# 128 bytes more ahead of the experts' token and activation buffers in a two-layer trunk (GLA, retention, SwiGLU, experts)

## The chip, the core and the metric

The kernel runs on one core of one Trainium2 chip. The metric is the device time of one execution in microseconds (us); lower is better. Three runs of the kernel before took 1833.35, 1835.13 and 1835.06 us, median 1835.06.

## What is computed

256 tokens of 1,024 features, with 16 learned meta tokens ahead of them (272 in all), go through two layers. Each layer has two attention-like branches merged by gates, a norm, then a channel mixer and a second norm. The mixer is a dense SwiGLU in the first layer and eight experts, of which each token uses two, in the second. Cut to the part that the change touches:

```python
def swiglu(x, w_gate, w_up, w_down):
    return (jax.nn.silu(x @ w_gate) * (x @ w_up)) @ w_down

def moe_swiglu(x, w_router, w_gate, w_up, w_down):
    t = x.reshape(-1, d)
    probs = jax.nn.softmax((t @ w_router).astype(jnp.float32), axis=-1)
    top_p, top_i = lax.top_k(probs, TOP_K)
    top_p = top_p / jnp.sum(top_p, axis=-1, keepdims=True)
    combine = jnp.sum(jax.nn.one_hot(top_i, N_EXPERTS) * top_p[..., None], axis=1)
    for e in range(N_EXPERTS):
        out = out + combine[:, e:e + 1] * swiglu(t, w_gate[e], w_up[e], w_down[e])
    return out
```

All inputs are float32. An expert's three matrices are 1024 x 3584, 1024 x 3584 and 3584 x 1024.

## The kernel before

**Split products.** Every large product is made of three float32r matmuls. An operand is split into a high half, which ScalarE (ACT) makes by a copy to float32r, and a low half, which VectorE (DVE) makes as operand less high half. `mm3` (lines 763 to 765) adds weights-low x stream-high, weights-high x stream-low and high x high into one PSUM tile. In the names of the trace, `ps<-w_hi,xg_lo` has the streamed tile first and the tile whose columns are loaded as weights second. "Loaded as weights" is meant here as TensorE's: the operand that LDWEIGHTS puts into the array.

**Units.** Weight matrices come from memory in units of 128 x 2048 float32 (1 MB). SyncE issues a load into one of `RAW` = 6 slots of `raw` when VectorE is done with the unit that was there (`lo_ready`). ACT writes the unit's high half into one of `HALVES` = 3 slots of `w_hi`, as soon as TensorE is done with the unit three before (`units_used`); VectorE then writes `w_lo`; TensorE waits for `lo_ready` before the unit's first matmul, and a unit is 12 matmuls of 512 columns in the experts.

**Dense stages** (layer 0, and layer 1 up to the router). The model's matrices are loaded as weights, 128 columns at a time (`w_hi`, `w_lo`), and the tokens are streamed: `hT`, `zT`, `mT`, `aT`, each with 272 columns, or with 256, which begin 16 columns (64 bytes) later.

**Experts.** The roles are swapped. An expert's tokens are gathered by one-hot matmuls into `xg_hi`, `xg_lo` (two experts per gather), and 128 of their columns at a time are loaded as weights, while 512 columns of the expert's matrix are streamed. The hidden dimension has 7 chunks of 512. A chunk of an expert is, on TensorE, in `chunk` (line 1139 and on): the gate, 2 units (24 matmuls, lines 763 to 765); the turn, four transposes of the activations `a_sl` of the chunk before (line 1086); the up, 2 units (24 matmuls, lines 763 to 765); and the down, 2 units (24 matmuls, lines 1101 to 1104), whose weights are the turned activations of the chunk before, `ag_hi` and `ag_lo`. After the turn, ACT does in program order: `ag_hi` (line 1231, called from `turned`), the gate's SiLU `g_sl` (line 1475), and then the `w_hi` of the two units of the down. VectorE does `ag_lo` (line 2107), the `w_lo` of the down's units (line 1820), and the product `a_sl` (line 2117) between them. There are 8 experts, so 56 chunks. Each engine's order is written out by hand, and nothing in it depends on addresses.

**Where the tiles lie.** Tensors are placed one behind another in each SBUF partition, each at the next multiple of 32 bytes. Three of the unnamed pads (`row_start`, `hidden_start`, `tokens_start`) only move what follows them. Byte addresses in a partition, from the built program:

| tile | role | address before | modulo 256 | after, modulo 256 |
|---|---|---|---|---|
| w_hi, w_lo (slots of 8,192) | weights in dense, stream in experts | 53,376; 77,952 | 128 | 128 |
| hT_hi, hT_lo (rows of 1,280 per k) | dense stream | 115,776; 126,016 | 64 | 64 |
| zT_hi, zT_lo (rows of 1,088 per k) | dense stream | 196,576; 205,280 | 224, 32, 96, 160 with k | same |
| aT_hi, aT_lo (rows of 1,280 per k) | dense stream (FFN) | 145,984; 174,144 | 64 | 64 |
| x_hi, x_lo | weights in the gathers | 145,984; 154,176 | 64 | 192 |
| S | stream in the gathers | 162,368 | 64 | 192 |
| xg_hi, xg_lo | weights in gate and up | 165,440; 173,632 | 64 | 192 |
| g_sl, a_sl | SiLU, activations | 181,824; 183,872 | 64 | 192 |
| ag_hi, ag_lo | weights in down | 185,920; 187,968 | 64 | 192 |
| y_hi, y_lo | stream in the last scatter | 190,016; 194,112 | 64 | 192 |

Steps within a tile are 2,048 bytes per k in w_hi and w_lo and 512 per k in xg and ag, all multiples of 256.

Of the kernel before, what the change touches and what calls it, by code (L numbers as in the profile page):

```python
# [28 lines left out]
P = 128  # L29
# [166 lines left out]
def trunk(nc, w, consts, where, out):  # L196

    ctx = ExitStack()
    with ctx:
# [3 lines left out]
        def sb(stack, name, shape, dt=F32):  # L203
            return stack.enter_context(nc.sbuf_tensor(name, shape, dt))
# [99 lines left out]


        moe = ExitStack()
        sb(moe, "tokens_start", [P, 24])
        x_hi = sb(moe, "x_hi", [P, 2, D], F32R)
        x_lo = sb(moe, "x_lo", [P, 2, D], F32R)
        S = sb(moe, "S", [P, 2, 2, P], F32R)  # L310
# [1983 lines left out]
```

How the kernel before makes its waits and increments, by code:

```python
        def landed(eng, u):  # L435
            eng.wait_ge(raw_landed[u % RAW], 16 * (u // RAW + 1))
# [2 lines left out]
        def hi_unit(act, u):  # L440
            landed(act, u)
            if u >= HALVES:
                act.wait_ge(units_used, u - HALVES + 1)
            k, n = shape_of(u)
            nc.scalar.activation(w_hi[:, u % HALVES, 0:k * n], raw[:, u % RAW, 0:k * n], ACT.Copy).then_inc(hi_ready, 1)
# [1 line left out]
        def lo_unit(dve, u):  # L447
            dve.wait_ge(hi_ready, u + 1)
            if u >= HALVES:
                dve.wait_ge(units_used, u - HALVES + 1)
            k, n = shape_of(u)
            if stream[u][0] == "twice":
                second = [unit(a, i, k, n).rearrange("p k (q i r) -> p (k q) i r", i=2, r=RANK)[:, :, 1, :] for a, i in ((w_hi, u % HALVES), (raw, u % RAW))]
                nc.vector.tensor_tensor(second[0], second[1], second[0].bitcast(F32), ALU.subtract).then_inc(lo_ready, 1)
                return
            nc.vector.tensor_tensor(w_lo[:, u % HALVES, 0:k * n], raw[:, u % RAW, 0:k * n],
                                    w_hi[:, u % HALVES, 0:k * n].bitcast(F32), ALU.subtract).then_inc(lo_ready, 1)
# [1 line left out]
        def lo_half(dve, u, q):  # L459
            if q == 0:
                dve.wait_ge(hi_ready, u + 1)
                dve.wait_ge(units_used, u - HALVES + 1)
            these = slice(q * UNIT // 2, (q + 1) * UNIT // 2)
            nc.vector.tensor_tensor(w_lo[:, u % HALVES, these], raw[:, u % RAW, these], w_hi[:, u % HALVES, these].bitcast(F32),
```

## Time and profile before

| what | value |
|---|---|
| median of the three runs | 1835.06 us |
| the profiled execution | 1834.15 us |
| its span, first to last instruction | 1832.1 us |
| TensorE matmuls | 10,888, busy 1792.3 us (98%) |
| VectorE | busy 1367.0 us (75%) |
| ScalarE | busy 1097.3 us (60%) |
| memory traffic | 498.61 MB, mean 272 GB/s |
| granted TensorE clock, mean | 0.993 of full speed |

The profile's page gives the busy time of every engine, a picture of the span in 40 slices, the chain of work that ended last, and the costliest groups of instructions with their mean durations. Matmuls are pipelined: their records overlap, so the pace of TensorE is read from the starts of neighbouring matmuls in the timeline and not from their durations. In the timeline the first column is the start in us from the start of the span, the second the duration.

### The profile page before, as it was taken

How to read it: one execution, taken by the hardware profiler on the slowest of the kernel's cores; microseconds unless marked ns; L12 is line 12 of the kernel's file. 1: busy time of each engine (PE TensorE's matmuls, PEld its weight loads, DVE VectorE, ACT ScalarE, POOL GpSimd, SP SyncE). 2: the span in 40 equal slices, each digit the busy share in tenths (PEclk: the TensorE clock that was granted, in tenths of full speed). 3: DMA queues.
4: the chain of work that ended last, by engine and by line, in shares of the span. 5: the costliest groups of instructions: out<-in, count | busy, mean ns of one | idle time of the engine just before them, and what ended most of it. 6: DMA issues, size and time to landing. Idle time of an engine off the chain costs nothing.

```text
span 1832.1 us, 28131 instructions
## 1 busy us (share of the span) xinstructions
PE 1792.3 (98%) x10888; PEld 1591.6 (87%) x10888; DVE 1367.0 (75%) x1159; ACT 1097.3 (60%) x840; POOL 74.3 (4%) x141
## 2 busy tenths in 40 slices
PE   8999999999999999999999999999999999999996
PEld 8999999999989999998878888888888888888875
DVE  4756577545457466668888888888888888888887
ACT  5544354543345442647777777777677777777774
POOL 0300200000003002000000000000000000000100
PEclk9999999999999999998999999999999999999998
DMA  8635443545535455344999999999999999999993
GB/s 334 209 133 168 163 162 138 184 148 186 185 138 194 150 187 187 131 175 164 370 364 380 366 347 379 364 381 379 348 369 369 365 383 372 349 371 371 397 395 131
DMA packets 75826, 498.61 MB, mean 272 GB/s; under 512 B 11072, under 2 KB 11584, under 8 KB 17872
## 3 DMA queue, kind: packets, MB, share of 16 engines
q1 hardware_dynamic: 68304, 482.38, 69.7%
q0 software_dynamic: 5824, 11.55, 2.0%
q10 hardware_dynamic: 1600, 3.31, 0.7%
q8 instruction: 69, 1.13, 0.3%
q14 instruction: 29, 0.24, 0.0%
HBM read 485.83 MB, written 4.72 MB: 268 GB/s over the span
## 4 chain that ended last, share of the span: by engine, by line
PE 55%; DVE 2%; issue 2%; ACT 1%; DVEq 0%; ACTq 0%
PE ps L763 12%; PE ps L765 12%; PE ps L764 12%; PE ps L1101 5%; PE ps L1103 5%; PE ps L1104 5%; PE ps L1086 1%; DVE w_lo L1820 1%; PE ps L1123 1%; ACT w_hi L1231 1%; PE ps L1034 0%; PE ps L1043 0%; PE ps L941 0%; PE ps L945 0%; DVE a_sl L2117 0%
## 5 line engine op out<-in xcount | busy, mean ns | idle before, releaser
L1820 DVE TENSOR_TENSOR w_lo<-raw,w_hi 128x2048 fp32r<-128x2048 f32 x336 | 762.8, 2289 | 127.2 <-ACT w_hi L1231 125.7
L1231 ACT ACTIVATE w_hi<-raw 128x2048 fp32r<-128x2048 f32 x336 | 638.3, 1918 | 177.6 <-PE ps L1104 89.6
L456 DVE TENSOR_TENSOR w_lo<-raw,w_hi 128x2048 fp32r<-128x2048 f32 (+2 forms) x126 | 272.5, 2171 | 195.2 <-ACT w_hi L445 194.6
L763 PE MATMUL ps<-hT_hi,w_lo 128*128 128x272 f32 (+1 forms) x1376 | 396.2, 288 | 15.4 <-DVE w_lo L456 8.1
L765 PE MATMUL ps<-hT_hi,w_hi 128*128 128x272 f32 (+1 forms) x1376 | 394.1, 286 | 0.0
L764 PE MATMUL ps<-hT_lo,w_hi 128*128 128x272 f32 (+1 forms) x1376 | 394.0, 286 | 0.0
L763 PE MATMUL ps<-w_hi,xg_lo 128*128 128x512 f32 x896 | 357.8, 399 | 2.4 <-DVE w_lo L1820 2.4
L765 PE MATMUL ps<-w_hi,xg_hi 128*128 128x512 f32 x896 | 351.3, 392 | 0.0
L764 PE MATMUL ps<-w_lo,xg_hi 128*128 128x512 f32 x896 | 350.1, 391 | 0.0
L445 ACT ACTIVATE w_hi<-raw 128x2048 fp32r<-128x2048 f32 (+2 forms) x130 | 234.2, 1807 | 179.2 <-PE ps L765 141.6
L763 PEld LDWEIGHTS ps<-hT_hi,w_lo 128*128 128x128 f32 x1376 | 261.1, 190 | 17.9 <-DVE w_lo L456 8.1
L764 PEld LDWEIGHTS ps<-hT_lo,w_hi 128*128 128x128 f32 x1376 | 261.1, 190 | 0.1
L765 PEld LDWEIGHTS ps<-hT_hi,w_hi 128*128 128x128 f32 x1376 | 261.0, 190 | 0.0
L765 PEld LDWEIGHTS ps<-w_hi,xg_hi 128*128 128x128 f32 x896 | 168.2, 188 | 38.9
L763 PEld LDWEIGHTS ps<-w_hi,xg_lo 128*128 128x128 f32 x896 | 168.5, 188 | 38.0 <-DVE w_lo L1820 2.5
L764 PEld LDWEIGHTS ps<-w_lo,xg_hi 128*128 128x128 f32 x896 | 168.5, 188 | 34.2
L1101 PE MATMUL ps<-w_hi,ag_lo 128*128 128x512 f32 x440 | 176.3, 401 | 0.0
L1103 PE MATMUL ps<-w_lo,ag_hi 128*128 128x512 f32 x440 | 172.5, 392 | 0.0
L1104 PE MATMUL ps<-w_hi,ag_hi 128*128 128x512 f32 x440 | 172.1, 391 | 0.0
L1101 PEld LDWEIGHTS ps<-w_hi,ag_lo 128*128 128x128 f32 x440 | 82.6, 188 | 28.0 <-DVE w_lo L1820 9.2
L1104 PEld LDWEIGHTS ps<-w_hi,ag_hi 128*128 128x128 f32 x440 | 82.6, 188 | 19.0
L1103 PEld LDWEIGHTS ps<-w_lo,ag_hi 128*128 128x128 f32 x440 | 82.7, 188 | 15.7
(306 smaller groups left out, 1813.0 us busy)
## 6 DMA issues: line engine op xcount, KB each, us to landing
raw<-in_dense_units SPq DMA_DIRECT2D x116, 1024.0 KB, 4.9
raw<-in_moe_w_gate SPq DMA_DIRECT2D x112, 1024.0 KB, 7.3
raw<-in_moe_w_up SPq DMA_DIRECT2D x112, 1024.0 KB, 7.1
raw<-in_moe_w_down SPq DMA_DIRECT2D x112, 1024.0 KB, 7.1
raw<-in_dense_units SPq DMA_DIRECT2D x10, 512.0 KB, 3.8
result_rows<-rows POOLq DMA_DIRECT2D x7, 512.0 KB, 8.6
v_tok<-turned_v POOLq DMA_DIRECT2D x48, 64.0 KB, 2.8
srT<-o_tok ACTq DMA_DIRECT2D x6, 272.0 KB, 4.6
```

The source lines that it names most:

```text
L445: nc.scalar.activation(w_hi[:, u % HALVES, 0:k * n], raw[:, u % RAW, 0:k * n], ACT.Copy).then_inc(hi_ready, 1)
L456: nc.vector.tensor_tensor(w_lo[:, u % HALVES, 0:k * n], raw[:, u % RAW, 0:k * n], w_hi[:, u % HALVES, 0:k * n].bitcast(F32), ALU.subtract) ...
L763: nc.tensor.matmul(dst, l_lo, r_hi, start=start, stop=False)
L764: nc.tensor.matmul(dst, l_hi, r_lo, start=False, stop=False)
L765: return nc.tensor.matmul(dst, l_hi, r_hi, start=False, stop=stop)
L1086: last = nc.tensor.transpose(TB[:, i * P:(i + 1) * P], a_sl[:, i * P:(i + 1) * P], ident)
L1101: last = nc.tensor.matmul(Y[:, q, :], a_lo[:, 2 * i + kk, :], u_hi[:, o:o + COLS], start=first and i == 0 and kk == 0, stop=False)
L1103: nc.tensor.matmul(Y[:, q, :], a_hi[:, 2 * i + kk, :], u_lo[:, o:o + COLS], start=False, stop=False)
L1104: last = nc.tensor.matmul(Y[:, q, :], a_hi[:, 2 * i + kk, :], u_hi[:, o:o + COLS], start=False, stop=final and i == 1 and kk == 1)
L1123: last = nc.tensor.matmul(ps[1 - half][:, 2 + k // 2, (k % 2) * 2 * P:(k % 2 + 1) * 2 * P], x_[:, t, f:f + P], S[:, t, :, :].rearrange("p ...
L1231: return nc.scalar.activation(dst, src, ACT.Copy, **kw)
L1820: tt(w_lo[:, at % HALVES, :], raw[:, at % RAW, :], w_hi[:, at % HALVES, :].bitcast(F32), ALU.subtract).then_inc(lo_ready, 1)
```

## The change

The pad ahead of the experts' buffers grows from 24 to 56 float32 per partition, so that all tensors that are allocated behind it in the experts' part of SBUF begin 128 bytes further on. Tensors of the dense stages, which share that memory at other times, and `raw`, `w_hi` and `w_lo` keep their addresses. No instruction is added, removed or moved on any engine.

```diff
         moe = ExitStack()
-        sb(moe, "tokens_start", [P, 24])
+        sb(moe, "tokens_start", [P, 56])
         x_hi = sb(moe, "x_hi", [P, 2, D], F32R)
         x_lo = sb(moe, "x_lo", [P, 2, D], F32R)
         S = sb(moe, "S", [P, 2, 2, P], F32R)
```

## Rows read from the trace of the kernel before

**Rows 1.** The page, busy time and share of the span.

```profile
span 1832.1 us, 28131 instructions
...
PE 1792.3 (98%) x10888; PEld 1591.6 (87%) x10888; DVE 1367.0 (75%) x1159; ACT 1097.3 (60%) x840; POOL 74.3 (4%) x141
```

**Rows 2.** Busy time by stage: PE, PEld, DVE, ACT, POOL, clock, DMA share, GB/s.

```profile
1000.00:1700.00 700.00, 700.00 (x3169) 570.99 (x3168) 605.04 (x348) 511.45 (x342) 2.67 (x5) 1.00 0.96 368
...
1700.00:1740.00 40.00, 40.00 (x179) 32.54 (x178) 34.89 (x20) 29.86 (x20) 8.85 (x5) 1.00 1.00 403
```

**Rows 3.** Timeline of PE, one chunk: down, gate, turn, up, next down.

```profile
1404.44 0.45 PE L1101 MATMUL ps<-w_hi,ag_lo 128*128 128x512 f32 x1
...
1405.88 0.39 PE L1101 MATMUL ps<-w_hi,ag_lo 128*128 128x512 f32 x1
...
1414.81 0.39 PE L763 MATMUL ps<-w_hi,xg_lo 128*128 128x512 f32 x1
...
1415.51 0.60 PE L1086 MATMUL ps<-tab,a_sl 128*128 128x128 f32 x4
...
1421.22 0.40 PE L765 MATMUL ps<-w_hi,xg_hi 128*128 128x512 f32 x1
1421.46 0.45 PE L1101 MATMUL ps<-w_hi,ag_lo 128*128 128x512 f32 x1
1421.75 0.39 PE L1103 MATMUL ps<-w_lo,ag_hi 128*128 128x512 f32 x1
```

**Rows 4.** Timeline of PE, the same instructions in another chunk.

```profile
1300.08 0.40 PE L1103 MATMUL ps<-w_lo,ag_hi 128*128 128x512 f32 x1
...
1309.41 0.40 PE L765 MATMUL ps<-w_hi,xg_hi 128*128 128x512 f32 x1
```

**Rows 5.** Timeline of PE, dense stages: ends of four stretches of 48 spacings.

```profile
57.84 0.28 PE L765 MATMUL ps<-hT_hi,w_hi 128*128 128x272 f32 x1
...
63.76 0.28 PE L765 MATMUL ps<-hT_hi,w_hi 128*128 128x272 f32 x1
...
627.75 0.28 PE L763 MATMUL ps<-hT_hi,w_lo 128*128 128x256 f32 x1
...
633.51 0.28 PE L763 MATMUL ps<-hT_hi,w_lo 128*128 128x256 f32 x1
...
265.93 0.29 PE L765 MATMUL ps<-zT_hi,w_hi 128*128 128x272 f32 x1
...
271.95 0.29 PE L765 MATMUL ps<-zT_hi,w_hi 128*128 128x272 f32 x1
...
775.81 0.28 PE L764 MATMUL ps<-zT_lo,w_hi 128*128 128x256 f32 x1
...
781.49 0.28 PE L764 MATMUL ps<-zT_lo,w_hi 128*128 128x256 f32 x1
```

**Rows 6.** The costliest groups: busy us, mean ns, idle before and its releaser.

```profile
L1820 DVE TENSOR_TENSOR w_lo<-raw,w_hi 128x2048 fp32r<-128x2048 f32 x336 | 762.8, 2289 | 127.2 <-ACT w_hi L1231 125.7
L1231 ACT ACTIVATE w_hi<-raw 128x2048 fp32r<-128x2048 f32 x336 | 638.3, 1918 | 177.6 <-PE ps L1104 89.6
...
L763 PE MATMUL ps<-w_hi,xg_lo 128*128 128x512 f32 x896 | 357.8, 399 | 2.4 <-DVE w_lo L1820 2.4
...
L1101 PE MATMUL ps<-w_hi,ag_lo 128*128 128x512 f32 x440 | 176.3, 401 | 0.0
```

**Rows 7.** Timelines of ACT, DVE and PEld from the turn to the down.

```profile
1416.15 0.60 ACT L1231 ACTIVATE ag_hi<-ps 128x512 fp32r<-128x512 f32 x1 [1.28 <-PE ps L1086]
1416.64 0.59 ACT L1475 ACTIVATE g_sl<-ps 128x512 f32<-128x512 f32 x1
1417.12 3.71 ACT L1231 ACTIVATE w_hi<-raw 128x2048 fp32r<-128x2048 f32 x2
...
1419.07 4.49 DVE L1820 TENSOR_TENSOR w_lo<-raw,w_hi 128x2048 fp32r<-128x2048 f32 x2 [1.27 <-ACT w_hi L1231]
...
1421.41 0.19 PEld L1101 LDWEIGHTS ps<-w_hi,ag_lo 128*128 128x128 f32 x1 [0.22 <-DVE w_lo L1820]
```

**Rows 8.** Waits from 850 us on: total us, times, longest.

```profile
PEld ps L1101 <- DVE w_lo L1820: 9.2, 42, 0.2
```

## The prediction

> **What bounds the kernel now.** I read the page first. TensorE's matmul row is busy for 98% of the span [rows 1], so time is to be looked for between one matmul's start and the next. Then the table by stage: from 1000 to 1700 us, inside the experts, PE is busy all 700 us at the full granted clock (1.00, which is the 2.4 GHz level), with VectorE at 605 us and DMA at 0.96 and 368 GB/s [rows 2]. A busy PE says nothing of its pace, because each matmul's record (about 0.39 us) overlaps the next. The pace is in the starts, so the third view is the timeline of one chunk of an expert. Call the distance from one matmul's start to the next its spacing. From 1405.88 to 1414.81 us there are 39 spacings: 8.93 us / 39 = 229.0 ns [rows 3]. The 512 streamed columns at 2.4 GHz are 213.3 ns, so 15.7 ns of each matmul is something else. In another chunk the same instructions go at 233.3 ns (1300.08 to 1309.41, 40 spacings in 9.33 us) [rows 4]: two steady paces for one code, 4.3 ns apart. Four of the 56 chunks go at the slower pace from down to gate; one stands here for them.
>
> The dense stages show what that rest may be. Four stretches of 48 spacings each [rows 5]: with hT streamed, 272 columns, 5.92 us / 48 = 123.3 ns, 10.0 over the 113.3 of its columns; with hT, 256 columns, 5.76 / 48 = 120.0, 13.3 over 106.7; with zT, 272 columns, 6.02 / 48 = 125.4, 12.1 over; with zT, 256 columns, 5.68 / 48 = 118.3, 11.6 over. Same engine, same kind of operand, same clock. What differs is where the operands lie. While one matmul streams, the next one's weights are loaded, so for each pair I take the **distance**: start address of the weights being loaded less the start of the columns being streamed, modulo 256 bytes. From the table of addresses it is +64 in the first stretch (128 - 64), 0 in the second (its stream begins 16 columns, 64 bytes, later), and goes round +160, +96, +32, +224 with k in the two of zT, whose rows of 1,088 bytes are no multiple of 256. In the experts the roles are swapped: the stream is w_hi or w_lo (128), the weights are xg or ag (64), the distance is -64, that is 192, and the rest is the largest of all, 15.7 or 20.0.
>
> The Trainium skill (TensorE: Matmul & The Clock Gate, Part 2, the step on LDWEIGHTS) says that PE has two independent read ports into SBUF, so that loading the next weights takes no read bandwidth from the running matmul, and its Part 1 gives a start to start of N / 2.4 GHz plus about 2.5 ns, 215.7 ns for 512 columns. By that rule addresses could not matter; the trace disagrees on the pace, with 229.0 ns.
>
> **The change, part by part.**
>
> 1. *No instruction is added, removed or moved.* Every engine's order is the same, and nothing ahead of the router touches a moved buffer: 0 us.
>
> 2. *The gates, ups and downs.* They are 56 chunks of 72 matmuls, 4,032 in all: 896 on each of the three lines of the gates and ups, and on each of the three lines of the downs 440 [rows 6] and 8 more of the last down, whose weights lie in xg. Their stream stays at 128, their weights go from 64 to 192, so the distance goes from 192 to +64, which is what the first stretch has now. No row shows 512 columns at +64. Bounds: the best neighbour is that stretch itself, 10.0 over, so 213.3 + 10.0 = 223.3 ns; the worst is the pace that these very matmuls already fall into, 233.3 ns. I take 225.0, that is 11.7 over: the mean of the four dense stretches (10.0, 13.3, 12.1, 11.6 make 11.75). I don't take 10.0, because two stretches that differ in columns and distance together can't tell me which of the two made the 10.0.
>
> 3. *What of it reaches the end.* A chunk is gate (24 matmuls), a turn of four transposes, up (24), down (24). From the turn at 1415.51 to the first down at 1421.46 PE does not set the time [rows 3]. The chain there is [rows 7]: the turn ends, ACT writes ag_hi from 1416.15, g_sl from 1416.64, then w_hi from 1417.12 (1.92 us for the first of the two [rows 6]), VectorE the w_lo of it from 1419.07 for 2.29 us [rows 6] to 1421.36, and the down's weight load starts at 1421.41 with 0.22 us of idle time ended by that w_lo. The waits add up to 9.2 us over 42 times [rows 8]. So an up phase that runs faster only waits longer: its 1,344 matmuls give nothing. The margin is thin: the first down comes 0.24 us after the last up matmul, one ordinary spacing, and its successor 0.29 us later in place of 0.23, so the wait costs PE about 0.06 us a chunk, 3.4 us in 56. The other 48 matmuls of a chunk (down, then gate) have no such tie: 1404.44 to 1415.51, 11.07 us. Their w_lo come in time: the table of waits has no other line by which w_lo holds PE for over 3 us of the stage.
>    Gain: 56 x 48 = 2,688 matmuls x (229.0 - 225.0) = 10.8 us, and the four slow chunks give 4 x 48 x 4.3 = 0.8 us more. **11.6 us**.
>
> 4. *Who must follow.* A chunk goes from 17.02 to 16.8 us. From 1000 to 1700 us VectorE is busy 605 of 700 us and ACT 511 [rows 2], which is 14.7 and 12.4 us of a chunk. Six units of 1.049 MB in 16.8 us are 374 GB/s, and from 1700 to 1740 us the queues moved 403 [rows 2]. I cost these at 0. If that cover failed, DMA kept at 368 GB/s would give the whole 11.6 back.
>
> 5. *The small ones.* The 224 transposes, 128 gathers and 8 scatter matmuls: in the gathers stream and weights (S and x) move together, distance 0 before and after. ACT and VectorE write ag, xg and a_sl at new places; nothing in the trace tells that an address matters to them. 0, with a bound of half a microsecond either way.
>
> Sum: span 1832.1 - 11.6 = 1820.5; the profiled execution took 1834.15, 2.05 over its span, so 1822.5; the median of the runs shown, 1835.06, lies 0.9 above that execution, so **1823.5 us**.
>
> **The rivals.**
>
> *Nothing changes.* The pattern of places may repeat every 128 bytes, and then +64 and -64 are one place; or the rest of 15.7 ns comes from the 512 columns and not from the distance. For it: hT's k step, 1,280 bytes, is a multiple of 128 as well as of 256, and the steady rows don't tell the two apart; 15.7 is outside what any dense stretch has, as if length had a part in it. Against: the two steady dense stretches differ by 3.3 ns, and zT's wander with k. Time: 1835. The Trainium skill's rule of the two read ports (same page and step) would end here too.
>
> *The slower pace becomes the usual one.* The stream and the load fall into step with each other, and the new distance may favour the step that now takes 4 chunks of 56. The 2,688 down and gate matmuls then take 233.3: 2,688 x 4.3 = 11.6, less 0.8 for the chunks that already do. The up phase becomes longer by 1,344 x 4.3 = 5.8, but the first 3.4 of it fills the wait for w_lo. Together +13.2 us: 1848. It decides from 230.4 ns on: 1.4 ns on 2,688 matmuls are 3.7 us, while the up phase's 1.9 still vanish in the wait. For it: the pace exists, with the same instructions. Against: it is the rarest in the trace, and the distance of the coming layout has the shortest rest in the dense stage.
>
> *The up phase was not pinned.* If the chain of ACT and VectorE shortened too, all 4,032 would gain 4.0 ns, 16 us, and 1818. Against it stands [rows 7]: none of the four durations depends on PE's pace.
>
> **How the numbers follow.** A measurement of this kernel can tell 0.2%, 3.7 us, from no change; in down and gate that is 1.4 ns a matmul. Faster by more, at 223 to 227 ns: 0.50, the up phase unpinned within it at 0.03. No change: 0.24. Slower: 0.26, of which the full slower pace is some 0.12 and a pace between 230 and 233 the rest. The forecast is the likeliest case, 1823.5. Its own range is 1818 (223.3 ns: 2,688 x 5.7 + 0.8 = 16.1) to 1831. The whole range has to reach into the slower cases, so 1817 to 1848.
>
> **What the profile after would show.** The time up to the first gate's matmul the same to 1 us. In a chunk, 39 spacings from down into gate in 8.78 us (225.0) and not 8.93. From the turn to the first down still 5.95 us, with the waits of the down's weight load for w_lo grown from 9.2 us to about 9.2 + 56 x 24 x 0.0040 = 14.6 us. VectorE's and ACT's mean durations unchanged (2.29, 1.92 us). DMA near 372 GB/s in the stage. Wrong would be: a chunk's spacings at 229.0 (no change), at 231 or more (the slower pace), or the time from turn to first down itself shorter.

## The result, and the profile after

| | before, same chip | after |
|---|---|---|
| median | 1834.38 us | 1845.07 us |
| lowest to highest, 4 runs each | 1833.35 to 1835.13 | 1843.73 to 1846.01 |
| the profiled execution, its span | 1834.15, 1832.1 | 1846.01, 1844.2 |

The change makes the kernel slower: the ratio is 1.0055, with a 95% interval of 1.0043 to 1.0068, that is 10.7 us in the difference of the medians. The forecast was 1823.5 us, faster; the sign was wrong. The time lies inside the stated range, 2.9 us under the 1848 of the rival "the slower pace becomes the usual one".

The page of the kernel after, its span, busy shares and three of its groups, beside [rows 1, 6]:

```profile
span 1844.2 us, 28131 instructions
...
PE 1804.6 (98%) x10888; PEld 1593.7 (86%) x10888; DVE 1367.0 (74%) x1159; ACT 1099.2 (60%) x840; POOL 74.4 (4%) x141
...
L1820 DVE TENSOR_TENSOR w_lo<-raw,w_hi 128x2048 fp32r<-128x2048 f32 x336 | 762.8, 2289 | 137.9 <-ACT w_hi L1231 137.2
L1231 ACT ACTIVATE w_hi<-raw 128x2048 fp32r<-128x2048 f32 x336 | 640.2, 1919 | 183.5 <-PE ps L765 92.9
...
L763 PE MATMUL ps<-w_hi,xg_lo 128*128 128x512 f32 x896 | 359.4, 401 | 1.9 <-DVE w_lo L1820 1.9
```

The same instructions, and VectorE's and ScalarE's durations are unchanged (2289 ns, 1919 ns): the new addresses of what they write cost them nothing. A matmul's record is as long as before, 401 ns against 399. Nothing on the page names the cause. It tells only that PE is busy 12.3 us longer in a span that is 12.1 us longer.

Busy time by stage of the kernel after (PE, PEld, DVE, ACT, POOL, clock, DMA share, GB/s):

```profile
1000.00:1700.00 700.00, 700.00 (x3133) 565.46 (x3132) 598.11 (x345) 506.31 (x337) 2.68 (x5) 1.00 0.95 363
1700.00:1740.00 40.00, 40.00 (x180) 32.09 (x178) 34.46 (x19) 29.19 (x21) 8.70 (x5) 1.00 0.98 388
```

Against [rows 2] the same 700 us hold 3,133 matmuls and not 3,169, at the same granted clock of 1.00. DMA moves 363 GB/s where it moved 368, and VectorE idles more: they follow.

Timeline of PE after, one chunk, with the same rows as [rows 3]:

```profile
1406.43 0.60 PE L1086 MATMUL ps<-tab,a_sl 128*128 128x128 f32 x4
...
1412.24 0.40 PE L765 MATMUL ps<-w_hi,xg_hi 128*128 128x512 f32 x1
1412.47 0.40 PE L1101 MATMUL ps<-w_hi,ag_lo 128*128 128x512 f32 x1
1412.71 0.39 PE L1103 MATMUL ps<-w_lo,ag_hi 128*128 128x512 f32 x1
...
1413.87 0.39 PE L1101 MATMUL ps<-w_hi,ag_lo 128*128 128x512 f32 x1
...
1422.96 0.40 PE L763 MATMUL ps<-w_hi,xg_lo 128*128 128x512 f32 x1
```

From 1413.87 to 1422.96 there are 39 spacings from down into gate: 9.09 us / 39 = 233.1 ns, where before it was 229.0. That is the slower pace of [rows 4], and now all chunks go at it: from the fourth spacing of a phase on, the mean is 233.3 ns in gates, ups and downs alike. From the turn to the first down it is 6.04 us and was 5.95. The second down follows the first by 0.24 us, close to an ordinary spacing, where it was 0.29: the wait for `w_lo` is gone. The chain around it, timelines of ACT, DVE and PEld after, beside [rows 7]:

```profile
1407.07 0.60 ACT L1231 ACTIVATE ag_hi<-ps 128x512 fp32r<-128x512 f32 x1 [1.32 <-PE ps L1086]
1407.57 0.59 ACT L1475 ACTIVATE g_sl<-ps 128x512 f32<-128x512 f32 x1
1408.04 3.75 ACT L1231 ACTIVATE w_hi<-raw 128x2048 fp32r<-128x2048 f32 x2
...
1409.99 4.49 DVE L1820 TENSOR_TENSOR w_lo<-raw,w_hi 128x2048 fp32r<-128x2048 f32 x2 [1.32 <-ACT w_hi L1231]
...
1412.34 0.19 PEld L1101 LDWEIGHTS ps<-w_hi,ag_lo 128*128 128x128 f32 x1
```

The down's weight load at 1412.34 shows no idle time, while VectorE had the `w_lo` ready at about 1412.28 (1409.99 + 2.29). The row of [rows 8], 9.2 us over 42 times, is no longer among the waits, and the later run "The change on top of it", which makes that `w_lo` earlier still, leaves turn to first down at 6.04. So ups that go slower have used up the slack of that chain and now set the time themselves.

**Where the 10.7 us came from.** I added up the spacings of the experts' matmuls over all chunks. A spacing goes to the phase of its first matmul. "All" is the three phases and the last down (6.0 us, not in the column of the downs); the turns (19.9 us before and after) and the gathers are left out:

| us | gates | ups | downs | all |
|---|---|---|---|---|
| before | 308.97 | 314.45 | 309.45 | 938.8 |
| after | 314.12 | 318.68 | 310.89 | 949.7 |
| difference | +5.2 | +4.2 | +1.4 | +10.9 |

The downs grow by only 1.4 us because in them the vanished wait pays back: at the first spacing of the downs 2.65 us over all chunks, at the last spacing of the ups 0.47. The other 1.3 of the span's 12.1 us lie ahead: the first expert matmul starts at 844.6 us before and at 845.9 after, and the gather ahead of it is late by the same 1.3 us already (842.68 and 843.93). In the kernels below, whose instructions up to there are the same, the first expert matmul starts anywhere from 843.5 to 845.5, in no order of the distances, so I take this part for scatter between executions.

### The profile page after: what moved, and what is told of

It reads as the page before. It is cut to its first block, busy times and chain, and to the rows that moved or that the text cites. A ratio compares the mean times of both kernels' runs of the same rounds, so it can differ in the third digit from the quotient of the medians.

```text
span 1844.2 us, 28131 instructions
## 1 busy us (share of the span) xinstructions
PE 1804.6 (98%) x10888; PEld 1593.7 (86%) x10888; DVE 1367.0 (74%) x1159; ACT 1099.2 (60%) x840; POOL 74.4 (4%) x141
## 4 chain that ended last, share of the span: by engine, by line
PE 55%; DVE 2%; issue 2%; ACT 1%; DVEq 0%; ACTq 0%
PE ps L763 12%; PE ps L765 12%; PE ps L764 12%; PE ps L1101 5%; PE ps L1103 5%; PE ps L1104 5%; PE ps L1086 1%; DVE w_lo L1820 1%; PE ps L1123 1%; ACT w_hi L1231 0%; PE ps L1034 0%; PE ps L1043 0%; PE ps L941 0%; PE ps L945 0%; ACT g_sl L1475 0%
## 5 line engine op out<-in xcount | busy, mean ns | idle before, releaser
L1820 DVE TENSOR_TENSOR w_lo<-raw,w_hi 128x2048 fp32r<-128x2048 f32 x336 | 762.8, 2289 | 137.9 <-ACT w_hi L1231 137.2
L1231 ACT ACTIVATE w_hi<-raw 128x2048 fp32r<-128x2048 f32 x336 | 640.2, 1919 | 183.5 <-PE ps L765 92.9
L764 PE MATMUL ps<-w_lo,xg_hi 128*128 128x512 f32 x896 | 353.8, 395 | 0.0
L445 ACT ACTIVATE w_hi<-raw 128x2048 fp32r<-128x2048 f32 (+2 forms) x130 | 234.2, 1807 | 180.0 <-PE ps L765 141.9
```

The lines of the kernel that those rows point to most:

```text
L445: nc.scalar.activation(w_hi[:, u % HALVES, 0:k * n], raw[:, u % RAW, 0:k * n], ACT.Copy).then_inc(hi_ready, 1)
L764: nc.tensor.matmul(dst, l_hi, r_lo, start=False, stop=False)
L1231: return nc.scalar.activation(dst, src, ACT.Copy, **kw)
L1820: tt(w_lo[:, at % HALVES, :], raw[:, at % RAW, :], w_hi[:, at % HALVES, :].bitcast(F32), ALU.subtract).then_inc(lo_ready, 1)
```

## The experiments

All times are medians beside runs of the kernel before on the same chip. "Distance" is, as in the prediction, the start of the weights being loaded less the start of the streamed columns, modulo 256 bytes; -64 stands for 192 here. Edits are against the kernel before unless the text says otherwise.

### Which property of the addresses counts

**One full period further.** The theory takes addresses modulo 256.

```diff
-        sb(moe, "tokens_start", [P, 24])
+        sb(moe, "tokens_start", [P, 88])
```

> The pad is 88 instead of 24 float32, so the experts' tiles begin 256 bytes further on than before, again at 64 modulo 256. Theory D (the pace of the 512-column matmuls depends on the distance modulo 256 between the start of the weights being loaded and the start of the columns being streamed): distance 192 as before, spacing 229 ns in most chunks and 233.3 in a few, time 1835 within 0.2%. If instead any move of these tiles costs (a boundary that is crossed, or a period longer than 256 bytes), the spacing stays at 233.3 ns and the time near 1845 us.

Measured: 1834.52 us beside 1835.06, ratio 1.000 (0.999 to 1.0009). The pace of a chunk is 229.0 again (1422.93 to 1431.86, 39 spacings). That the tiles lie further on does nothing; 128 bytes more make the loss, 256 bytes more undo it.

**Everything 128 further.** Stream and weights move together, so the distance stays -64 while every place modulo 256 is a new one.

```diff
+        sb(ctx, "all_start", [P, 32])
         raw = sb(ctx, "raw", [P, RAW, UNIT])
```

> A pad of 32 float32 ahead of raw moves every tile by 128 bytes, streams and weights alike; tokens_start is 24 as before. The experts' weights now lie at 192 modulo 256 as in the changed kernel, and their streams at 0. Theory D (distance): every distance is as before, so 229 ns in the experts, 123.3 and 120.0 in the dense stretches, time 1835 within 0.2%. Theory A (the absolute place of the weights' tile, 192 instead of 64, sets the pace): 233.3 ns in the experts and 1845 us.

Measured: 1835.07 us beside 1835.06, ratio 1.0001 (0.9991 to 1.001), pace 229.0. It is the distance between the two operands, and not the place of either. This is the run that bears out step 2's choice of variable.

**The turned activations alone.** Only `g_sl`, `a_sl`, `ag_hi`, `ag_lo` and what lies behind them move; gates and ups keep -64, downs get +64.

```diff
         xg_lo = sb(moe, "xg_lo", [P, 2, KT, P], F32R)
+        sb(moe, "hidden_half_start", [P, 32])
         g_sl = sb(moe, "g_sl", [P, COLS])
```

> A pad of 32 float32 behind xg_lo moves g_sl, a_sl, ag and all behind them by 128 bytes, while x, S and xg stay. Distance +64 in the downs alone. Theory D: downs at 233.3 ns, gates and ups at 229 (unless a gate keeps the pace that the down before it fell into, as nothing stops PE between them; the up begins afresh after the turn and tells it). Time between: about a third of the 10.7 us, 1838; two thirds if the gates keep the downs' pace, 1842. If the moved writes of ACT and VectorE (g_sl, a_sl, ag) and not TensorE's reads made the loss, the whole of it, 1845, at unchanged gates.

Measured: 1840.02 us beside 1835.06, ratio 1.0028 (1.0018 to 1.0038). In the timeline of PE of this run the pace changes inside one chunk, at the line between down and gate (its lines are numbered one higher):

```profile
1409.21 0.39 PE L1102 MATMUL ps<-w_hi,ag_lo 128*128 128x512 f32 x1
...
1413.88 0.39 PE L1105 MATMUL ps<-w_hi,ag_hi 128*128 128x512 f32 x1
...
1414.81 0.39 PE L764 MATMUL ps<-w_hi,xg_lo 128*128 128x512 f32 x1
...
1419.39 0.39 PE L766 MATMUL ps<-w_hi,xg_hi 128*128 128x512 f32 x1
```

Twenty spacings each: 4.67 / 20 = 233.5 ns in the downs, whose weights moved, and 4.58 / 20 = 229.0 in the gates, whose weights did not. It is so in most chunks, but not in all. Of the 53 downs that a gate follows directly, all go at 233 ns; of the gates behind them 37 go at 229, 15 at 233 and one between, where in the kernel before 4 go at 233. So a gate can keep the slower pace of the down ahead of it although its own distance has not changed, as the expectation allowed for. By the sum over starts that makes the gates 1.3 us longer, which fits a time between its 1838 and 1842. Behind a turn, the ups are at 229 in all 56 chunks.

**The tokens alone.** The change, and behind `xg_lo` another 128 bytes, which bring the activations back to where they were modulo 256.

```diff
-        sb(moe, "tokens_start", [P, 24])
+        sb(moe, "tokens_start", [P, 56])
...
         xg_lo = sb(moe, "xg_lo", [P, 2, KT, P], F32R)
+        sb(moe, "hidden_half_start", [P, 32])
```

> The complement of e3: x, S and xg at 192 modulo 256 as in the changed kernel, g_sl, a_sl and ag put back to 64 by a second pad of 32 behind xg_lo. Distance +64 in gates and ups, -64 in downs. Theory D: gates and ups at 233.3 ns, downs at 229 and partly at 233.3 where they keep the pace; the up phase 4.3 us longer in sum as in the changed kernel, the gates 5.2, less the wait at the first down (3.1): about 6 us, 1841. With e3's 5.0 that adds up to the change's 10.7. If xg's writers or the gathers made the loss, gates and ups stay at 229.

Measured: 1841.61 us beside 1834.14, ratio 1.0037 (1.0024 to 1.005). By the sum over starts the gates are 5.0 us longer and the ups 4.3, while the downs are 2.4 shorter, since their wait is gone and their pace stayed at 229.6 (229.3 before). The two halves cost 1.0028 and 1.0037 where the whole costs 1.0055: the effect follows the operand, but for the gates that keep their downs' pace in the run above.

### Which distance does what

**The map.** Behind the last scatter, extra matmuls run in groups of 48 (16 times `mm3`) on tiles that are there anyway; nothing of the output comes from them. The weights start at a place in `hT` that is chosen per group, the stream starts at the start of `w_hi` and `w_lo`.

```diff
+            def pace(off, n, triples=16):
+                x_h, x_l = hT_hi[:, 1, off:off + P], hT_lo[:, 1, off:off + P]
+                for i in range(triples):
+                    mm3(ps[0][:, 0, 0:n], x_h, x_l, w_hi[:, 0, 0:n], w_lo[:, 0, 0:n], start=(i == 0), stop=(i == triples - 1))
+            for n in (512, 272, 256):
+                for off in range(0, 64, 8):
+                    for _ in range(2):
+                        turned_idle()
+                        pace(off, n)
```

> Behind the last scatter PE runs 48 stretches of 48 matmuls: 512, 272 and 256 columns streamed from w_hi and w_lo (128 modulo 256), weights from hT_hi and hT_lo at eight starts 32 bytes apart, distances -64, -32, 0, +32, +64, +96, +128, +160, each twice, four transposes ahead of each. It is extra work at the end, some 0.5 ms; the output is the same. Theory D: the spacing depends on the distance and repeats what the kernel shows: 512 columns 229 at -64 and 233.3 at +64, 272 columns 123.3 at +64, 256 columns 120.0 at 0. If length alone made the experts' larger rest, 512 columns would have one spacing at all eight. The map says whether a distance with under 229 ns exists.

Six stretches of its timeline of PE, 39 spacings each. In this order: 512 columns at the distances -64, 0 and +64, then 272 columns at +64, then 256 columns at 0 and at +64.

```profile
1838.90 0.39 PE L765 MATMUL ps<-w_hi,hT_hi 128*128 128x512 f32 x1
...
1847.83 0.40 PE L765 MATMUL ps<-w_hi,hT_hi 128*128 128x512 f32 x1
...
1873.61 0.39 PE L765 MATMUL ps<-w_hi,hT_hi 128*128 128x512 f32 x1
...
1882.45 0.40 PE L765 MATMUL ps<-w_hi,hT_hi 128*128 128x512 f32 x1
...
1919.60 0.39 PE L765 MATMUL ps<-w_hi,hT_hi 128*128 128x512 f32 x1
...
1928.70 0.40 PE L765 MATMUL ps<-w_hi,hT_hi 128*128 128x512 f32 x1
...
2063.76 0.29 PE L765 MATMUL ps<-w_hi,hT_hi 128*128 128x272 f32 x1
...
2068.57 0.29 PE L765 MATMUL ps<-w_hi,hT_hi 128*128 128x272 f32 x1
...
2139.45 0.28 PE L765 MATMUL ps<-w_hi,hT_hi 128*128 128x256 f32 x1
...
2144.12 0.28 PE L765 MATMUL ps<-w_hi,hT_hi 128*128 128x256 f32 x1
...
2170.13 0.28 PE L765 MATMUL ps<-w_hi,hT_hi 128*128 128x256 f32 x1
...
2174.55 0.28 PE L765 MATMUL ps<-w_hi,hT_hi 128*128 128x256 f32 x1
```

8.93 / 39 = 229.0; 8.84 / 39 = 226.7; 9.10 / 39 = 233.3; 4.81 / 39 = 123.3; 4.67 / 39 = 119.7 (120.0 by unrounded times); 4.42 / 39 = 113.3 ns. The whole map, in ns of a spacing over the time of the columns at 2.4 GHz (two values where the two repeats differ by over half a ns):

| distance | 512 columns | 272 | 256 |
|---|---|---|---|
| -64 | 15.6 or 20.0 | 13.3 | 11.1 |
| -32 | 20.0 | 12.5 | 10.0 |
| 0 | 13.3 | 12.1 | 13.3 |
| +32 | 20.0 | 12.0 or 13.3 | 11.7 |
| +64 | 20.0 | 10.0 | 11.1 or 6.7 |
| +96 | 20.9 | 9.9 | 12.1 or 10.7 |
| 128 | 19.9 or 19.1 | 13.3 | 12.0 |
| 160 | 20.0 | 12.0 | 13.3 |

The 20.0 at -64 is its first repeat. It began while the granted clock was at 0.50, the 1.2 GHz level, with matmuls 427 ns apart; when the clock rose in it, the rest of the group settled at 233.4 ns (1828.21 to 1836.38, 35 spacings), and the second repeat, begun at the full clock, at 229.0. So the two paces of [rows 4] and [rows 3] are there for one distance in this run too. That the beginning of a stretch decides between them is a guess from this one pair; the first repeat also had the last of the kernel's DMA traffic beside it (71 GB/s from 1828 to 1838 us, then none). This is the table that the prediction needed. Its column for 272 columns agrees with the dense stage, where +64 is among the best, 10.0 as in [rows 5]. Its column for 512 has another order: there +64 is as bad as nearly all others, -64 is the second best, and 0 is the best. The kernel before sat on one of the two good places that this map has at its own length, and the change moved it off.

**Other lengths.** The same extra work at 512, 448, 384, 320 and 256 columns, with 160 transposes ahead of the first group.

> A second map behind the last scatter, each stretch of 48 matmuls twice, 40 turns of transposes ahead so that the clock is up: 512 columns at distances -64, -48, -16, 0, +16, +48, +64, and 448, 384, 320 and 256 columns at -64, 0, +64. Extra work at the end; the output is the same. Open is why +64 gives 10.0 ns over the columns at 272, 11 or 6.7 at 256 and 20.0 at 512. Theory L1: the length modulo 64 columns (256 bytes) decides with the distance; then 448, 384 and 320 give 512's rests (15.6, 13.3, 20.0). Theory L2: the rest grows with the length, because the stream and the load disturb each other over a part of the stream; then +64 goes from about 11 at 256 to 20 at 512 through values between. If distances of 16 bytes either side of 0 are above 13.3, 0 is a narrow optimum; if below, a better place than 0 exists.

| over the columns, ns | -64 | 0 | +64 |
|---|---|---|---|
| 512 | 15.6 | 13.3 | 20.0 |
| 448 | 13.3 | 16.0 or 20.0 | 15.5 |
| 384 | 13.3 | 13.3 | 16.7 |
| 320 | 13.3 | 13.3 | 13.4 |
| 256 | 11.1 | 13.3 | 6.7 |

At 512 columns -48 gave 18.6, -16 gave 13.3 in one repeat and 15.0 in the other, and +16 and +48 20.0. I had thought of the columns' number modulo 64 as what turns the order round; all but 272 are multiples of 64 here and still don't agree, so that idea fell. At +64 the rest grows from 6.7 at 256 columns to 20.0 at 512, with 448 out of line. No simple rule in length and distance holds for the whole table. The values between 256 and 512 columns speak for a rest that grows with the length at this one distance, as theory L2 of the expectation has it, and against L1. At -64 it grows too (11.1, 13.3, 15.6), but at 0 it is 13.3 at every length except 448. Two repeats of the same group can settle at different paces here also. At -64 and 512 columns both repeats took 228.9 ns this time.

**Distance 160 in the kernel.** Is it the sign of the distance, or are -64 and 0 special? The tokens' tiles go to 32 modulo 256, so the distance is -96, that is 160.

```diff
-        sb(moe, "tokens_start", [P, 24])
+        sb(moe, "tokens_start", [P, 16])
```

> The pad is 16: the experts' tiles at 32 modulo 256 and not at 64, distance -96, that is +160. The map gave 233.33 ns there. Theory D with the map: the chunks at 233.3 and the time like the changed kernel's, 1845. If it is only the sign of the distance that matters (weights behind their stream good, ahead of it bad), -96 should be like -64, 229 ns and 1835.

Measured: 1845.53 us beside 1834.54, ratio 1.006 (1.0045 to 1.0076), pace 233.3 (1413.57 to 1422.67). It moves the tiles by 32 bytes and costs as much as the change does with 128. The map's 20.0 at 160 holds in the kernel.

**Distance 0 in the kernel.** The best place of the map.

```diff
-        sb(moe, "tokens_start", [P, 24])
+        sb(moe, "tokens_start", [P, 40])
```

> The pad is 40: the experts' tiles begin 64 bytes further on than before, at 128 modulo 256 like their streams, distance 0. Theory D with the map: 226.7 ns in place of 229.0 in down and gate, 2,688 x 2.3 = 6.2 us and 0.8 from the slow chunks; the up phase is pinned by the chain ACT, VectorE, down (turn to first down stays 5.95 us) and gives nothing: about 1828 us. If the up phase was not pinned, 10.1 us, 1825. A theory in which any step away from 64 harms, or in which the changed kernel's loss came from something else than the distance, gives 1835 or more.

Measured: 1828.91 us beside 1834.14, ratio 0.997 (0.9959 to 0.9982). Timeline of PE of this run, from down into gate, then the following turn:

```profile
1418.60 0.39 PE L1101 MATMUL ps<-w_hi,ag_lo 128*128 128x512 f32 x1
...
1427.44 0.39 PE L763 MATMUL ps<-w_hi,xg_lo 128*128 128x512 f32 x1
...
1428.12 0.60 PE L1086 MATMUL ps<-tab,a_sl 128*128 128x128 f32 x4
...
1434.03 0.50 PE L1101 MATMUL ps<-w_hi,ag_lo 128*128 128x512 f32 x1
1434.37 0.39 PE L1103 MATMUL ps<-w_lo,ag_hi 128*128 128x512 f32 x1
```

39 spacings in 8.84 us: 226.7 ns, the map's number. The first down comes 5.91 us behind the turn and was at 5.95; the second comes 6.25 behind it and was at 6.24. So what the chain of `w_lo` holds in place is the second down, not the first: the mean from the turn to the second down, over the 50 chunks whose turn, up, down and next gate follow without a gather between, is 6.25 us in the kernel before and 6.25 here. The wait has grown; its row among the waits from 850 us on:

```profile
PEld ps L1101 <- DVE w_lo L1820: 10.7, 42, 0.3
```

This is step 3 of the prediction in a kernel that did become faster. By the sums, gates win 3.5 us, ups only 1.4, and downs 0.6, since their first spacing now takes 316 ns at the median and took 292: over all chunks 1.5 us more, which is all that the ups won. The ups win less than 24 x 2.3 ns a chunk for a reason of their own, too: 28 of the 56 go at 231 ns for about their first ten spacings and at 227 from then on, and with the wait taken away (below, distance 0 and the swap) 27 do so still.

### What the wait for w_lo costs

**The wait taken away alone.** ACT makes the high half of the down's first unit ahead of the gate's SiLU and that of the second behind it; `w_lo` is then ready before the down needs it.

```diff
                     turned(k - 1, uj)
+                    hi_of(g, 8, turns, uj + 4)
                     silu(k, uj + 2)
-                    for i in range(4, 6):
-                        hi_of(g, 4 + i, turns, uj + i)
+                    hi_of(g, 9, turns, uj + 5)
```

> The kernel before with the swap of e6 alone, tiles at 64. Theory P: the up phase keeps its 229 ns and only the wait at the first down goes, 3.4 us: 1831.6. The difference between e4 to e6 and this one is then what the pin took from a shorter spacing. Against P: no change, 1835.

Measured: 1828.2 us beside 1834.14, ratio 0.9968 (0.9956 to 0.998). The timeline of PE around the end of the ups:

```profile
1412.49 0.60 PE L1086 MATMUL ps<-tab,a_sl 128*128 128x128 f32 x4
...
1418.21 0.39 PE L765 MATMUL ps<-w_hi,xg_hi 128*128 128x512 f32 x1
1418.44 0.39 PE L1101 MATMUL ps<-w_hi,ag_lo 128*128 128x512 f32 x1
1418.67 0.39 PE L1103 MATMUL ps<-w_lo,ag_hi 128*128 128x512 f32 x1
```

The second down comes 0.23 us after the first. From the turn to the first down it is 5.95 us as in the kernel before: with the wait gone, turn and ups alone take that long. To the second down it is 6.18 in place of 6.24. The wait was priced at 3.4 us and the edit gives 5.9. By position within the phases, over all chunks, the wait itself shows as 3.2 us at the first spacing of the downs, 0.8 at the last of the ups, and 0.5 at the second and third of the downs: 4.5 us. Another 1.0 us lies at the step from the down to the gate, and there nearly all of it in four places: 1268, 820, 817 and 1025 ns became 1065, 493, 495 and 815. The first three are gates that wait for their own `w_lo`, the fourth is the step to the last down. So the swap shortens other waits with the first. The row of the gates' wait before, and in this run:

```profile
PE ps L763 <- DVE w_lo L1820: 2.4, 5, 0.9
```

```profile
PE ps L763 <- DVE w_lo L1820: 1.0, 2, 0.7
```

The rest is in ordinary spacings, of which fewer go at the slower pace (in the downs a mean of 228.9 ns, and 229.3 before).

**The change on top of it.** With the slack gone, nothing should absorb a slower up.

```diff
-        sb(moe, "tokens_start", [P, 24])
+        sb(moe, "tokens_start", [P, 56])
...
                     turned(k - 1, uj)
+                    hi_of(g, 8, turns, uj + 4)
                     silu(k, uj + 2)
-                    for i in range(4, 6):
-                        hi_of(g, 4 + i, turns, uj + i)
+                    hi_of(g, 9, turns, uj + 5)
```

> The changed kernel (pad 56, distance +64) with the swap of e6. Theory: in the changed kernel the wait at the first down was already gone, so the swap gives it nothing: 1845. Against e7, the same at distance -64, the loss is then that of all 4,032 matmuls with nothing absorbed, 4,032 x 4.35 = 17.5 us (1828.2 to about 1845.5), where the change alone cost 10.7. If the swap helps by another way than the wait, it gives some 6 us here too, 1839.

Measured: 1842.94 us beside 1834.54, ratio 1.0049 (1.0033 to 1.0064). Against the run before it, which has the swap alone, the ratio is 1.0049 / 0.9968 = 1.0081, 14.9 us, where the change alone costs 10.7. So the wait hid about 4 us of the slower pace. The 17.5 us of the expectation were too many, since it counted every spacing of every phase. By the sum over starts the two kernels differ by 15.6 us, and the first three spacings of the ups are no slower in this one. With the slower pace the swap is worth next to nothing: 1.0049 and 1.0055 have intervals that overlap. In the trace it still gives 1.3 us at the same four steps out of a down.

### The version that beats both

**Distance 0 and the swap.** The two edits of above together.

> e4, and in ScalarE's chunk the SiLU is issued behind the first w_hi of the down and not ahead of it. Theory P (the up phase is pinned by ag_hi, SiLU, w_hi, w_lo): that w_lo is ready some 0.5 us sooner, the wait at the first down goes, 0.06 us x 56 = 3.4 us, and the up phase gains 1,344 x 2.3 = 3.1 us of its own: about 6.5 us below e4, 1821 to 1822. If e4 shows the up phase unpinned, or if the chain is held by something else (ag_lo on VectorE, the load), no gain over e4.

Measured: 1819.1 us (1819.0 to 1820.64) beside 1834.14, ratio 0.992 (0.9906 to 0.9933). Its timelines of PE and of ACT:

```profile
1408.60 0.60 PE L1086 MATMUL ps<-tab,a_sl 128*128 128x128 f32 x4
...
1414.53 0.39 PE L1101 MATMUL ps<-w_hi,ag_lo 128*128 128x512 f32 x1
1414.75 0.39 PE L1103 MATMUL ps<-w_lo,ag_hi 128*128 128x512 f32 x1
...
1425.41 0.60 PE L1086 MATMUL ps<-tab,a_sl 128*128 128x128 f32 x4
```

```profile
1409.23 0.60 ACT L1231 ACTIVATE ag_hi<-ps 128x512 fp32r<-128x512 f32 x1 [1.24 <-PE ps L1086]
1409.72 1.91 ACT L1231 ACTIVATE w_hi<-raw 128x2048 fp32r<-128x2048 f32 x1
1411.54 0.58 ACT L1475 ACTIVATE g_sl<-ps 128x512 f32<-128x512 f32 x1
```

Turn to first down 5.93 us, to the second 6.15, first down to next turn 10.88, where the kernel before has 5.95, 6.24 and 11.07. In ACT's rows the `w_hi` stands ahead of `g_sl`, which puts the down's `w_lo` 0.5 us earlier. The gains of the two edits alone, 0.3% and 0.3%, give 0.8% together: each uncovers what the other left. The expectation had 1821 to 1822; it counted the wait at 3.4 us.

**The dense stream moved too.** On top of that version `hT` begins 32 bytes earlier modulo 256.

```diff
-        sb(ctx, "row_start", [P, 48])
+        sb(ctx, "row_start", [P, 40])
...
-        sb(ctx, "after_a2", [P, 48])
+        sb(ctx, "after_a2", [P, 56])
```

> e6 and hT_hi, hT_lo 32 bytes nearer (row_start 40, after_a2 56): distance +96 where hT streams 272 columns and +32 where 256. The map: 123.3 ns at +96 like at +64, and 118.4 at +32 in place of 120.0 at 0. Theory D: the 864 matmuls of layer 1 with hT and 256 columns save 1.6 ns each, 1.4 us: 1817.7, under what the measurement tells; the trace's spacings tell it. If the dense stretches have other causes, their spacings stay at 123.3 and 120.0.

Measured: 1818.99 us beside 1834.54, ratio 0.9915 (0.9902 to 0.9929): no difference from the version above that these runs can tell. The pace of the 256-column stretches went from 119.9 to 118.3 ns, so the lever works there also, but those stretches make up too little of the span.

## Why the prediction was wrong, by its own steps

- **Step 1, nothing moved:** held. The page counts 28131 instructions in both, and all durations off TensorE are the same.
- **Step 2, the choice of variable:** held. The distance modulo 256 between loaded weights and stream is what counts: one period further nothing changes, both moved together nothing changes, and each tile of weights moved alone changes its own matmuls, with the one exception of the 15 gates that kept their downs' pace. The rival "nothing changes", by either of its two ways, fell.
- **Step 2, the value, is the step that failed.** "I take 225.0, that is 11.7 over: the mean of the four dense stretches." It measured 233.3. The mean was taken over stretches of 256 and 272 columns and carried over to 512, as if the rest depended on the distance alone. The maps show that the order of the distances is another one at each length: +64 is the best or next to it at 272 and 256 columns (10.0; 11.1 or 6.7) and as bad as nearly all others at 512 (20.0). My own sentence, that two stretches which differ in columns and distance together can't tell me which of the two made the 10.0, was the warning; the mean made of them has the same flaw. The nearest row was the upper bound, [rows 4]: the same instructions at the same length. Reading it as a rare accident at this distance, and not as the pace of most distances at 512 columns, was the error of weight; and that -64 at 512 already had the largest rest of all rows made me take a good place for a bad one.
- **Step 3, the up phase is pinned:** held in its effect, and seen in both directions, but not at the place that the step names. It says that PE does not set the time from the turn to the first down. It does: that time is 5.96 us in the mean with the wait and 5.95 without it. Held is the second down, 6.25 us behind the turn. A faster pace (distance 0) leaves that at 6.25 us, brings the first down a little nearer (5.96 to 5.93) and lets the wait grow from 9.2 to 10.7. A slower pace first eats the wait, and then sets the time: 6.04 us to the first down. So "turn to first down still 5.95" was no test of the pin.
- **Step 3, the price of the wait:** mis-sized. 3.4 us was read from one chunk's first spacing; summed over all chunks, that spacing, its two followers and the last of the ups lost 4.5 us to it. The edit that takes it away gave 5.9, because it shortens other waits too: 1.0 us at the steps out of the downs, most of it gates that wait for their own `w_lo`.
- **Step 4, the followers:** held in the direction that came to be tried by the best version. It moves 372 GB/s in the stage at 0.96 DMA share, above the 368 of before, and the queues did not hold it.
- **Step 5:** held within its bound, as far as the noise of 3 us ahead of the first expert matmul lets one see.
- **The range:** 223.3 ns and its 16.1 us give 1835.1 - 16.1 = 1819, not the 1818 of the text; nothing else hangs on it.
- **The rival of the slower pace** came true. Its price was 13.2 us: 11.6 less 0.8 in downs and gates, 5.8 less 3.4 in the ups. Measured: 10.9 by the sum over starts. Its pace was right (233.3). It counted all 24 spacings of each phase, and the first three of a phase hardly change (0.2 us or less over all 56 chunks at nearly each of them), so the slower pace itself is 14.3 us and not 16.6; the wait took back 3.4 of it, as stated, if the few tenths behind the first down are counted in.
- **The rule of the Trainium skill** (TensorE: Matmul & The Clock Gate, Part 2, the step on LDWEIGHTS), by which the load takes no bandwidth from the running matmul, gave no change. The runs show 226.7, 229.0 and 233.3 ns for the same instruction, by address alone, and none comes near the 215.7 that its Part 1 gives. Here the measurement decides. That loads and streams meet at something with a period of 256 bytes is what these runs are consistent with; what it is, no run shows.

**What stays open.** Why the number of columns changes the order of the distances, why one distance can settle at either of two paces, and what decides between them. The maps show both and explain neither, and whether other types than float32r behave so was not tried.

## What to carry to other kernels

Where, as here, every float32r matmul has its own weight load, the start of the weights against the start of the stream, modulo 256 bytes, is a tuning knob, at 512 columns worth 3% of TensorE's pace (226.7 to 233.3 ns), at no instruction; pads of 32 bytes turn it, and both operands must be held in place while other tiles are moved. Map it with the kernel's own number of columns, since a good distance at 272 columns is a bad one at 512. And when a pace changes, first find the waits behind it: here one of them took two fifths of what a faster pace gives (5.2 us with it, 0.992 / 0.9968 or 9 us without), hid about 4 us of a slower one, and cost 4.5 us by itself.

## What the hardware showed that I had not expected

- At 512 columns, of all distances tried, only 0, -16 (13.3 to 15.0 ns over the columns), -64 (15.6 as a rule) and -48 (18.6) are clearly better than about 20; 32 bytes (distance -64 to 160) can cost 4.3 ns a matmul, 11 us here.
- Many of the paces come in steps. 113.3, 120.0, 123.3, 126.7, 146.7, 173.3, 200.0, 226.7 and 233.3 ns are all multiples of 3.33 ns, 8 cycles at 2.4 GHz. Others, as steady, are not: 117.8, 125.4, 202.2, 229.0, 232.0 and 234.2. Summed by position over the 56 chunks, the ups before repeat by three (226.5, 228.9 and 231.3 ns) and after by two (235.0 and 231.6 ns), although the code repeats by three in both.
- A wait that one chunk's first spacing shows as 0.06 us costs 0.08 us in the mean over the chunks (4.5 us / 56), since the neighbours of the late matmul are late too.
- The distance alone does not fix the pace of a stretch. A gate behind a slow down can stay slow (15 of 53), and half of the ups at distance 0 begin at 231 ns and settle at 227.
